# Mixers of a hybrid block: two turned steps of the sparse attention one behind the other, their value products two by two

## The reference, cut to what matters

```
def block(inp):                       # 128 queries, 4 heads of 64, one key and value head for all
    ...
    _, sel = lax.top_k(score, n_sel)
    ...
    logits = jnp.einsum('bthd,btkd->bhtk', qb, kg).astype(f32)
    bias = jnp.moveaxis(rel_bias_dsa[rel_bucket(dist)], -1, 1)
    logits = jnp.where(valid[:, None], logits + bias, -jnp.inf)
    probs = jax.nn.softmax(logits, axis=-1).astype(vg.dtype)
    return jnp.einsum('bhtk,btkd->bthd', probs, vg)
```

## Time and profile before

| | |
|---|---|
| median of 3 runs | 2831.82 us |
| lowest and highest | 2830.13 and 2831.91 us |
| profiled execution, span | 2830.9 us |
| PE, DVE, ACT, POOL busy over the whole span | 2596.2, 1813.7, 1283.1, 922.8 us |
| stretch of the mixers | about 845 to 1356 us |

### The profile page before, as it was taken

The page is one execution under the profiler, slowest core; times in us unless marked ns, Lnnn a source line. Parts: engine busy times, 40 slices in busy tenths (PEclk is TensorE's granted clock), DMA queues, the critical chain, the costliest instruction groups (busy, mean ns, idle before and its releaser), DMA issues. The chain is left out here.

```text
span 2830.9 us, 34992 instructions
## 1 busy us (share of the span) xinstructions
PE 2596.2 (92%) x10908; PEld 1642.9 (58%) x10909; DVE 1813.7 (64%) x2566; ACT 1283.1 (45%) x2400; POOL 922.8 (33%) x925
## 2 busy tenths in 40 slices
PE   6988779999987899898799979999999999998998
PEld 3634323344863445444688756666666666665787
DVE  2176999699977788876333486644644444743676
ACT  2277867967956676766321222222222222222322
POOL 2377877700011111121000043434444444433221
PEclk9999989999997899999899989999999999999999
DMA  5101131113152123222544459975776665973663
GB/s 151 63 33 42 32 58 38 35 63 98 38 169 78 62 73 102 76 71 74 200 143 143 177 224 356 351 273 210 282 270 227 237 223 201 347 286 138 198 216 132
DMA packets 221474, 438.08 MB, mean 155 GB/s; under 512 B 22888, under 2 KB 91048, under 8 KB 221224
## 3 DMA queue, kind: packets, MB, share of 16 engines
q1 hardware_dynamic: 199400, 357.78, 36.8%
q0 software_dynamic: 13312, 47.32, 5.3%
q10 hardware_dynamic: 8640, 31.46, 2.7%
HBM read 331.14 MB, written 105.38 MB: 154 GB/s over the span
## 5 line engine op out<-in xcount | busy, mean ns | idle before, releaser
L2504 DVE CAST p_high<-p_low 128x2048 fp32r<-128x2048 f32 x128 | 203.0, 1586 | 400.4 <-PE p_psG L2611 293.3
L698 PE MATMUL p_psP<-home,p_ring 128*128 128x512 f32 x832 | 366.3, 598 | 0.0
L2627 PE MATMUL p_psY<-p_wd,p_hT 128*128 x752 | 330.9, 593 | 2.4 <-ACT p_hT L2686 2.2
L2506 DVE TENSOR_TENSOR p_low<-p_low,p_high 128x2048 fp32r<-128x2048 f32 x128 | 318.9, 2492 | 4.4
L698 PEld LDWEIGHTS p_psP<-home,p_ring 128*128 128x128 f32 x832 | 157.3, 191 | 205.0 <-issue 204.9
L2627 PEld LDWEIGHTS p_psY<-p_wd,p_hT 128*128 128x128 f32 x752 | 139.3, 190 | 160.6 <-issue 160.4
L727 PE MATMUL p_psI<-p_kI,p_qI 64*128 64x512 f32 (+3 forms) x608 | 148.1, 596 | 62.9 <-ACT p_relu L589 62.8
L2547 POOL TENSOR_TENSOR p_xT_low<-p_xT,p_xT_high 128x512 fp32r<-128x512 f32 x94 | 186.1, 1998 | 3.4 <-ACT p_xT L2671 3.4
L2609 PE MATMUL p_psG<-p_high,p_xT_high 128*128 128x512 f32 x376 | 167.2, 445 | 15.8 <-DVE p_low L2506 8.2
L2553 POOL TENSOR_TENSOR p_hid<-p_act_g,p_act_u 128x512 f32<-128x512 f32 x47 | 62.2, 1324 | 307.7 <-ACT p_act_u L2681 294.8
L603 ACT ACTIVATE p_relu<-p_relu,p_small 128x512 f32<-128x512 f32 (+3 forms) x266 | 161.5, 662 | 0.0
(11 more groups left out here) (423 smaller groups left out, 5833.4 us busy)
## 6 DMA issues: line engine op xcount, KB each, us to landing
p_low<-in_w_expert_gate_dram SPq DMA_DIRECT2D x32, 2048.0 KB, 13.5
p_low<-in_w_expert_up_dram SPq DMA_DIRECT2D x32, 2048.0 KB, 18.3
p_wd<-in_w_expert_down_dram SPq DMA_DIRECT2D x32, 2048.0 KB, 10.7
y_dram<-p_y ACTq DMA_DIRECT2D x47, 512.0 KB, 8.1
p_xt<-in_x_dram SPq DMA_DIRECT2D x32, 512.0 KB, 4.7
y_dram<-p_clear SPq DMA_DIRECT2D x32, 512.0 KB, 4.3
proj_f<-p_stage SPq DMA_DIRECT2D x52, 256.0 KB, 2.4
p_ot<-o_dram SPq DMA_DIRECT2D x16, 512.0 KB, 4.5
```

Source lines behind the costliest of these rows:

```text
L698: mm = pe.matmul(psP[0:n, i % 2, :], w, aT[:, k, c * CH:(c + 1) * CH], start=k == 0, stop=k == KD - 1)
L2504: dve.tensor_copy(high[:, m, k, :], low[:, par, m, k, :].bitcast(F32)).then_inc(high_done, 1)
L2506: dve.tensor_tensor(low[:, par, m, k, :], low[:, par, m, k, :].bitcast(F32), high[:, m, k, :].bitcast(F32), ALU.subtract).then_inc(w_split, 1)
L2627: mm = pe.matmul(psY[:, c, :], hT[:, k, :], wd[:, bass.ds(at, 1), k, c * CH:(c + 1) * CH].rearrange("p a f -> p (a f)"), start=k == 0, sto ...
```

## The change

The loop over the steps of a unit takes two steps at a time where the unit has more than two. Both T items are put into the list one behind the other; then O, then the next unit's Q that both steps were to bring, then the V items, of which all but two are taken out at once, so they too come in pairs; then P, and the E items that fell to either step. The time `slot` moves on by both steps together. An odd last step stays single, and units of one or two steps are as before. No instruction is added or removed, and no tile, bank count or semaphore changes; bank numbers follow from the new order.

```
-            for sp in range(n):
-                slot += 1 + 1.5 / n
+            for sp in range(0, n, 2 if n > 2 else 1):
+                both_now = range(sp, min(sp + 2, n)) if n > 2 else range(sp, sp + 1)
+                slot += (1 + 1.5 / n) * len(both_now)
                 now = []
                 if sp == 0:
                     at = len(ahead) if n <= 2 else min(1, len(ahead))
                     now += ahead[:at]
-                now.append(("T", u, sp))
+                now += [("T", u, s) for s in both_now]
 
                 while behind and behind[0][0] == "O":
                     now.append(behind.pop(0))
-                upto = max(at, min(len(ahead), -(-len(ahead) * (sp + 1) * 2 // n)))
+                upto = max(at, min(len(ahead), -(-len(ahead) * (both_now[-1] + 1) * 2 // n)))
                 now += ahead[at:upto]
                 at = upto
-                behind.append(("V", u, sp))
-                if sp == n - 1:
+                behind += [("V", u, s) for s in both_now]
+                if n - 1 in both_now:
                     behind += [("P", u), ("O", u)]
 
                 while sum(b[0] == "V" for b in behind) > 2:
...
                 if u + 1 < NU:
-                    now += [("E", u + 1, h) for h in range(2) if sp == max(0, n - 3 + h)]
+                    now += [("E", u + 1, h) for h in range(2) if max(0, n - 3 + h) in both_now]
```

## The result

The changed kernel takes 2837.7 us (median of 18 runs, 2834.3 to 2842.4) against 2831.9 us before (18 runs): a ratio of 1.0021, 95% interval 1.0015 to 1.0028. It is **slower by 5.8 us**, where 2823.5 us, a gain of 8, was forecast; the time lies just inside the range, on the wrong side. The profiled execution's span is 2835.5 us.

What follows compares the result with a forecast made beforehand. PE was taken to bound the mixers by a small margin. Terms of -12.2 (shape changes), -5.1 (relief at O and o) and +9.0 (lumps) summed to -8.3 us, giving 2823.5 us, range 2814 to 2838.

Steps and rivals of the forecast that it cites:

- PE is the bound by a small margin: Mixers, 900 to 1356 us: PE busy 402.9 of 456 us, DVE 353.3, ACT 310.6; not the bound everywhere.
- Fewer changes of shape, -14.4 us: PE's item order: 50 more 128*128 neighbours, 57 more 128*64 and 12 more 64*128 save 14.4 us.
- Both prices of 0.10: PE saving in us per V-V neighbourhood, from one row, and per 64*128 neighbourhood, taken as for V.
- The first rival: PE's saving is hidden by waits or DVE becomes the bound: about 2832.5 us, chance 0.20.
- 15% of it lost where PE waits or DVE is full: Mixers: 12% for PE's idle time and about 4% for DVE's full piece cut 14.4 to 12.2 us.
- T pairs, PT, psO, banks, at nothing: Pairs in the mixers: buffer waits and distance between a bank's fill and next use hardly change; no cost.
- O further behind P: Two T between a unit's last V and its O: shorter waits at O and o, 10.2 us, half counted, -5.1.
- The other streams in lumps, +9.0 us: Window blocks: v at 2, 6, 15 and o at 9 lose cover and wait 2.5, 4.0, 1.5, 1 us for ACT.
- The sign of being wrong that was named: PE's idle time up by over 12 us, at T for L1405 or L1395, would point to the second rival.
- Both E in one run, at nothing: ACT, 12 units: both exponentials together, 3 to 5.3 us, covered by over 6 us of PE work; no cost.
- the second rival: Both E together outrun PE's cover in 12 units: 2849 us in full, 2839 if half is felt; chance 0.15.
- Six sevenths of the forecast's own range faster by over 5.7 us: Chances: most of the range 2816 to 2830 counted as faster; with the third rival, faster 0.58.

Runs made afterwards that it cites:

- e3: The changed kernel, but the other streams' items also fall between each pair's T T O Q and its V V P E; 2815.8 us.
- e5: e3 with only the linear stream's items moved back ahead of the T pair, the window's left spread; 2810.9 us.
- e9: The changed kernel, but within a lump the first v or o and what follows it in its stream go between T pair and V pair; 2811.4 us.
- e1: The kernel before, T and V kept single, with the window and linear items in lumps between every second step; 2854.2 us.
- e7: e3 with one V of each pair moved to the other side of the items between, so V stands single; 2831.1 us.
- e12: The changed kernel with v of window blocks 2, 6, 15 and o of block 9 set back ahead of the next V pair; 2824.9 us.
- e2: The kernel before with only both E of the next unit placed together, as the changed kernel has them; 2834.0 us.
- e4: The changed kernel with E set between the two T of a pair where it followed that step before, in units of four and more steps; 2842.3 us.
- e10: The kernel before, no pairs, with v of blocks 2, 6, 15 right behind its turned probabilities and o of block 9 right behind v; 2842.4 us.

## Why the prediction was wrong, point by point

- **PE is the bound by a small margin: right.** In e3, 17.1 us less work on PE at the same idle time made the kernel 16.2 us faster.
- **Fewer changes of shape, -14.4 us: right in kind, a little small.** e3, with 127 fewer changes of shape (463 to 336) where the changed kernel has 119 fewer, measures 17.1 us. Both prices of 0.10 were too small: a second V gains too (1.02 us for two, so 0.15), and so does a second Q. Two Q of 512 keys take 1.92 us from start to start at the full clock, where nothing is waited for, against 1.06 for one, which saves 0.20:

```profile
1082.48 1.99 PE L1495 MATMUL p_psX<-p_kA,near 64*128 64x512 f32 x8
1084.40 1.08 PE L1517 MATMUL p_psO<-p_PT,p_small 128*64 128x256 f32 x8
```

  In one place of e3, e5 and e9 such a pair took 2.10 us and gained next to nothing. The first rival, by which the saving isn't one, is refuted.
- **15% of it lost where PE waits or DVE is full: wrong.** In e3 the kernel is 16.2 us faster and the stretch 18 us shorter for 17.1 us of work saved, about 5% lost at most. The 4% for the piece in which DVE was busy 47.1 of 50 us follows from no row, and nothing shows that piece as a bound. DVE's share of the stretch was 76% in the changed kernel and not the 79% expected.
- **T pairs, PT, psO, banks, at nothing: right**, by e3, whose idle time is 52.2 us against 53.1 before.
- **O further behind P: right at O** (8.2 to 0.5 us), **wrong at o.** The two long waits at o that were named did shrink (7.1 to 4.6, 1.7 to none), but others grew, and o in all went from 12.5 to 16.8. Half of the relief, 5.1 us, was counted; but pairs without lumps (e3) have waits of 8.7 us at O, and lumps without pairs (e1) 9.4, so neither alone brings this relief. It is a matter of how the streams happen to fall.
- **The other streams in lumps, +9.0 us: this is the step that failed.** The mechanism, the places and even the first prices were right: v2, v6, v15 and o9 were put at 2.5, 4.0, 1.5 and 1.0 and waited 2.9, 3.6, 2.7 and 2.6, together 11.8. What was wrong is the sum: the term stopped at the four that lost all cover, and it counted waits alone. The lumps cost 22 us in both arrangements, about two thirds of it idle time of PE and a third more busy time. Waits at v and o together went from 13.7 to 28.9 us, 15.2 more. The four are 11.8 of these, less the 0.3 that o9 waited before. The others make up the rest: o1, o5, o8, o13, v4 and v9 by 8.0 us, while o14 and o15 fell by 4.3. The sign of being wrong that was named, idle time up by over 12 us, came true (15.6), but at v and o and not at T.
- **The clock was left out.** Behind a wait PE may go on at about half its pace, though not behind each: the longest wait at a v (3.58 us, to 1078.53) was followed by a granted clock of 1.00 up to 1144 us. In the changed kernel PE waited 1.39 us before 1221.46, in a stretch that had run at a granted clock of 1.00; from 1222 to 1227 us it was 0.66, with two T taking 1.90 us. This follows:

```profile
1221.46 1.08 PE L1609 MATMUL p_psX<-home 128*128 128x64 f32 x8 [1.39 <-ACT p_PTW L1429]
...
1223.05 1.89 PE L1495 MATMUL p_psX<-p_kA,near 64*128 64x512 f32 x4
1224.87 1.96 PE L1506 MATMUL p_psX<-ident,p_logits 128*128 128x128 f32 x8
1226.77 1.13 PE L1495 MATMUL p_psX<-p_kA,near 64*128 64x512 f32 x4
```

  Over the stretch the clock went from 0.96 to 0.94. PE's busy time fell only by 9.6 us in the changed kernel where e3, with the same pairs, has 17.1: the difference is 7.5 us, of which e3's 8 fewer changes of shape (336 against 344) explain about 1. Weighted by the granted clock as for e7, PE's busy time comes to 370.3 us at full clock in the changed kernel and 366.8 in e3. So about 4 of the 7.5 us are work at the lower level of the clock (1.2 in place of 2.4 GHz). This is an estimate, no run tested it by itself, and 2 to 3 us stay open. e1 shows the same without pairs: 410.7 us busy against 402.9. Part of that is its 13 more changes of shape, about 2 us.
  The busy time doesn't simply follow the idle time: e12 has 11.3 us less idle time than the changed kernel, and PE is still busy 391.6 us at a clock of 0.94. Which waits bring the clock down stays open.
- **Both E in one run, at nothing: right** as far as can be measured, and with it the second rival is refuted as a mechanism, though its sign came true. e2 is 1.9 us slower within its interval; parting them again (e4) made it worse.
- **Six sevenths of the forecast's own range faster by over 5.7 us: a slip.** Of the 14 us from 2816 to 2830, only 10 lie below 2826.1. If the chance is spread evenly over them, faster loses some 0.08 of its 0.58.

In one line, the kernel's time: forecast -12.2 for the pairs and +3.9 for everything else; measured -16 and +22.

## What to carry to other kernels

When a planner interleaves several streams, widening the grain of one of them also coarsens the places at which the others may stand. Look for the dependent pairs of the *other* streams that become neighbours (multiply, copy on another engine, multiply), and list the cover of every one of them before and after beside the work that the copying engine has queued ahead, not only of those that lose it entirely. A sum over all would not do: in e10 the o behind each moved v gains the cover that the v loses, and the kernel is still 10 us slower. No run here tried such a list as a forecast. Four moved items cost 10 us here, about two thirds of the 16 us that 60 T pairs and 62 V pairs gained, and giving the other streams a place inside the pair kept the whole gain.

## What the runs showed of the hardware

- Two neighbouring items of the same array shape save about 0.15 us at full clock for 128\*128 and for 128\*64 (1.02 us for two and not 1.17), and mostly 0.20 us for two Q of 64\*128 (1.92 us and not 2.12).
- A wait of PE costs more than its length where the clock falls behind it: after one of 1.39 us two T took 1.90 us in place of 1.02. In the whole stretch 17.1 us of work saved (e3) became 9.6 (changed), at a granted clock of 0.95 and 0.94, by estimate half of it through the clock. The fall didn't come behind every wait, not even behind the one of 3.58 us.
- ACT's order among its own items (exponentials in one run, or a copy between them) moved the time by under 2 us in two of three trials and by 4.6 us in the third, which stays unexplained.
